# Softmax attention of a long fused kernel: the products for the maxima of a head run two heads ahead of its scores, and its row of maxima is made in the middle of the head before

## The reference, cut to what matters

```python
def block_attention(q, k, v):
    ...
    scale = dh ** -0.5

    def one_block(qi):
        sc = jnp.einsum("bqgrd,bkgd->bgrqk", qi, k).astype(jnp.float32) * scale
        p = jax.nn.softmax(sc, axis=-1).astype(v.dtype)
        return jnp.einsum("bgrqk,bkgd->bqgrd", p, v)
```

## Time and profile before

| | |
|---|---|
| median of 3 runs | 1560.02 us (1559.63 to 1560.45) |
| the profiled execution | 1560.5 us |
| its span, first to last instruction | 1558.7 us |
| TensorE busy | 98% of the span |
| VectorE, ScalarE, GpSimd busy | 73%, 54%, 58% |
| granted TensorE clock, mean | 0.998 of full |

### The profile page before, as it was taken

One profiled execution on the slowest core, in us unless ns is written; L12 is line 12 of the kernel. 1 busy time (PEld: TensorE's weight loads), 2 busy tenths in 40 slices (PEclk: granted clock), 3 DMA queues, 4 the chain that ended last, 5 costly groups with the idle time before them and its releaser, 6 DMA issues.

```text
span 1558.7 us, 23051 instructions
## 1 busy us (share of the span) xinstructions
PE 1528.3 (98%) x7975; PEld 1235.0 (79%) x7975; DVE 1139.1 (73%) x1590; ACT 834.7 (54%) x1552; POOL 907.3 (58%) x644
## 2 busy tenths in 40 slices
PE   7999999999999999999999999999999999999998
PEld 4778888888878766687777888888888888888887
DVE  4799888888739888488459878877768895567542
ACT  4775765766633587423344444444458665454442
POOL 0556765766655876556846767776753467532314
PEclk9999999999999999999999999999999999999999
DMA  8434434434332300276622333333422334322212
GB/s 328 133 122 129 128 108 130 131 107 129 115 94 70 81 28 1 83 239 249 214 67 83 96 92 103 108 109 109 113 83 81 95 102 122 94 62 69 68 41 82
DMA packets 77485, 171.34 MB, mean 110 GB/s; under 512 B 8321, under 2 KB 10753, under 8 KB 73921
## 3 DMA queue, kind: packets, MB, share of 16 engines
q1 hardware_dynamic: 70064, 133.09, 28.7%
q10 hardware_dynamic: 7312, 36.83, 6.7%
HBM read 167.67 MB, written 2.23 MB: 109 GB/s over the span
## 4 chain that ended last, share of the span: by engine, by line
PE 64%; DVE 13%; issue 8%; POOL 6%; DMA 2%; ACT 2%; ACTq 0%; DVEq 0%; POOLq 0%; SPq 0%
PE bank L1401 8%; PE bank L1403 7%; PE bank L1402 7%; PE bank L1419 7%; PE bank L1422 7%; PE bank L1420 7%; POOL w_lo L716 6%; PE bank L1864 4%; DMA w_raw<-ws 2%; PE bank L1866 2%; DVE ada_acc L2155 2%; PE bank L1757 2%; DVE rstd L2454 2%; PE bank L2021 1%; PE bank L1695 1%
## 5 line engine op out<-in xcount | busy, mean ns | idle before, releaser
L716 POOL TENSOR_TENSOR w_lo<-w_raw,w_hi 128x512 fp32r<-128x512 f32 x440 | 644.8, 1489 | 403.2 <-ACT w_hi L775 402.8
L775 ACT ACTIVATE w_hi<-w_raw 128x512 fp32r<-128x512 f32 x444 | 260.4, 624 | 124.0 <-DMA w_raw<-ws 104.2
L1401 PE MATMUL bank<-a_hi_and_lo,w_hi 128*128 128x512 f32 (+1 forms) x800 | 315.8, 395 | 2.4 <-ACT gates_early L840 1.2
L1403 PE MATMUL bank<-a_hi_and_lo,w_lo 128*128 128x512 f32 (+1 forms) x800 | 308.7, 386 | 0.0
L1402 PE MATMUL bank<-a_hi_and_lo,w_hi 128*128 128x512 f32 (+1 forms) x800 | 308.3, 385 | 0.0
L1419 PE MATMUL bank<-b_hi,w_hi 128*128 128x512 f32 x536 | 210.2, 392 | 2.6 <-ACT tmp L1119 1.4
L1422 PE MATMUL bank<-b_lo,w_hi 128*128 128x512 f32 x536 | 209.2, 390 | 0.0
L1420 PE MATMUL bank<-b_hi,w_lo 128*128 128x512 f32 x536 | 209.0, 390 | 0.0
L1401 PEld LDWEIGHTS bank<-a_hi_and_lo,w_hi 128*128 128x128 f32 x800 | 150.4, 188 | 36.6 <-issue 4.4
L1402 PEld LDWEIGHTS bank<-a_hi_and_lo,w_hi 128*128 128x128 f32 x800 | 150.5, 188 | 30.8 <-issue 1.9
L1403 PEld LDWEIGHTS bank<-a_hi_and_lo,w_lo 128*128 128x128 f32 x800 | 150.3, 188 | 30.8
(11 more groups left out here) (447 smaller groups left out, 3183.2 us busy)
## 6 DMA issues: line engine op xcount, KB each, us to landing
w_raw<-ws SPq DMA_DIRECT2D x457, 256.0 KB, 2.7
cs_rows<-cs_scratch ACTq DMA_DIRECT2D x16, 1024.0 KB, 5.2
ada_piece<-ada ACTq DMA_DIRECT2D x16, 1024.0 KB, 5.3
ada_piece<-ada SPq DMA_DIRECT2D x8, 1024.0 KB, 17.6
x_stream<-x SPq DMA_DIRECT2D x2, 1024.0 KB, 8.5
x_stream<-x ACTq DMA_DIRECT2D x1, 2048.0 KB, 7.8
out<-x_stream SPq DMA_DIRECT2D x4, 256.0 KB, 3.3
out<-x_stream SPq DMA_DIRECT2D x8, 128.0 KB, 1.8
```

Source lines behind the costliest of these rows:

```text
L716: nc.gpsimd.tensor_tensor(wlo[b][:, :], full[:, :], r32(whi[b][:, :]), ALU.subtract)\
L775: A(whi[n % RING][:, :], full[:, :], ACT.Copy).then_inc(hi_done, 1)
L1401: mm(out, lh, rh, start=first, stop=False)
L1403: return mm(out, ll, rh, start=False, stop=last)
```

## The change

Three edits, on four engines' lists:

- scores_for_max and max_of run for head h + 2 in head h (AHEAD_OF), except in heads 0 and 1, where it is h + 1 as before. The four M of head 3, which no head's chunks would hold, are put between the value products of heads 0 and 1. So heads 14 and 15 hold no M.
- row_of_max(h + 1) stands in the middle of head h, between its second and third chunk, for heads 2 to 14, and max_row(h + 1) on ScalarE between the third and the fourth exponential.
- query_high(3) moves into head 0 on ScalarE, and query_low(3) into head 0 on VectorE.

```diff
+AHEAD_OF = [1, 1] + [2] * (N_Q - 2)
...
                     A(probs_of(h)[:, c, :], S[n % 2][:, :], ACT.Exp, scale=HD ** -0.5).then_inc(exp_done, 1)
+                    if c == 2 and 1 < h < N_Q - 1:
+                        max_row(h + 1)
+                    if (h, c) == (0, 1):
+                        query_high(3)
                 if h % 2 == 0:
...
-                    max_row(h + 1)
                     if h == 0:
+                        max_row(1)
...
                 else:
-                    query_high(3)
+                    max_row(2)
                 if h + 3 < N_Q:
                     query_high(h + 3)
-                if h + 1 < N_Q:
-                    max_row(h + 1)
...
                     scores(h, c)
-                    if h + 1 < N_Q:
-                        scores_for_max(h + 1, c)
+                    if h + AHEAD_OF[h] < N_Q:
+                        scores_for_max(h + AHEAD_OF[h], c)
...
-                chunks_of(h, 0, NCH)
+                chunks_of(h, 0, NCH // 2)
+                if 1 < h < N_Q - 1:
+                    row_of_max(h + 1)
+                chunks_of(h, NCH // 2, NCH)
                 if h % 2 == 0:
                     take_sums(u - 1, 0)
-                    row_of_max(h + 1)
                     take_sums(u - 1, 1)
                     continue
...
                     values(u, c)
-                    if c == 1:
-                        if h + 1 < N_Q:
-                            row_of_max(h + 1)
-                        if u:
-                            turn_inverse(u - 1)
+                    if u == 0:
+                        scores_for_max(3, c)
+                        if c == 1:
+                            row_of_max(2)
+                    elif c == 1:
+                        turn_inverse(u - 1)
...
             for h in range(N_Q):
-                if h + 1 < N_Q:
+                if h + AHEAD_OF[h] < N_Q:
                     for i in range(NCH):
-                        max_of(h + 1, i)
+                        max_of(h + AHEAD_OF[h], i)
+                if h == 1:
+                    for i in range(NCH):
+                        max_of(3, i)
...
-                if h == 1:
+                if h == 0:
                     query_low(3)
```

## The result

The changed kernel takes **1566.2 us** (median of 8 runs, 1563.2 to 1570.2), the kernel before beside it 1560.5 us (8 runs, 1559.6 to 1564.5). The ratio is 1.0034, 95% interval 1.0024 to 1.0043: slower by 5.3 us by the ratio, by 5.8 between the two medians. The sum had +4.3 and the time 1564.3, the range 1561.3 to 1566.4. The profiled execution took 1566.2 us, span 1564.4, 5.7 more than before.

A forecast was written before the change was run, and what follows sets the result against it. TensorE, almost never waiting in the attention, was taken to bound the kernel. Terms 0.3 + 1.4 + 2.9 + 0.5 - 0.8 = +4.3 us moved the median from 1560.02 to 1564.3, range 1561.3 to 1566.4.

The forecast's parts named there:

- Head 4's query is wanted in head 2: Head 2's first M of head 4 waits 2.8 us for query_low(4), and the next matmul is 0.1 longer: +2.9 us.
- The M of head 3 between values: Four M among pair 0's values cost two at 0.47 and two at 0.24, for distances and changes of kind: +1.4 us.
- The row moved: Row among scores: -0.05 us in each of six even heads (2 to 12), +0.10 in six odd (3 to 13): +0.3.
- Heads 6 and 10: Query behind turn_q: head 6's new 0.9 us wait replaces an old 0.5, +0.4; head 10 +0.1; together +0.5.
- Head 14: Head 14 loses its four M, is paced by exponentials and hides the row: 4.99 to 4.15 us, -0.8.
- the chance for the clock: Rival: the clock falls to 1.2 GHz after head 2's pause, costing 1.8 us more: +6.1, 1566.1 us; chance 0.07.
- the delay would be absorbed behind the attention: Rival: waits of 1.2 and 1.5 us after the attention take up delay, leaving +1.6, 1561.6 us; chance 0.10.

The follow-up runs named there:

- the run with the clock kept: Changed kernel plus 15 bf16 matmuls of 384 columns between head 2's first scores and head 4's first M: 1565.4 us, ratio 1.0026 to the kernel before.
- the run with the row at the end: Changed kernel, head 1's reciprocal in head 0, query_low(4) before head 3's last reduction, row_of_max and max_row back in old places from head 2: 1561.8 us, ratio 1.0009.
- the version with VectorE moved: Kernel before, TensorE's order untouched, VectorE's reciprocals of the last two query tiles in heads 0, 5, 7 and turn_q in heads 3, 8: 1564.9 us, ratio 1.0023.

## Why the prediction came out as it did

The direction and the place were right, and the time was 1.9 us too low. The range held it by 0.2 us, and that is luck: its upper end was made for a fall of the clock of 1.8 us, and two more executions of the changed kernel took 1569.0 and 1570.0. By its own steps, in the attention:

- *Head 4's query is wanted in head 2*, +2.9: measured 2.8 and 0.1 (head 2 as a whole, in the run with the clock kept, 7.71 against 4.98). Its chain was right as well: reduction, 1.75 for the reciprocal, q_lo in 0.62 and not 1.27, with GpSimd idle from 554.81 on. One reading was too kind: the q_lo of 0.69 runs from 556.85 to 557.54, so GpSimd, at work from 557.08 on, worked for two thirds of it, and it was hardly slower than the 0.62. The rule on the shared SBUF interfaces (the Trainium skill, GPSIMD Engine Reference, Specifications) agrees in direction: 0.62 with GpSimd idle, 1.27 with GpSimd at work for nine tenths of it; but the 0.69 shows that work beside it need not cost much.
- *The M of head 3 between values*, +1.4: **measured +1.8** (head 2's first scores 19.59 behind the attention's start, before 17.77). I had priced a lone M at 0.47; the rows of the changed kernel have the last value products ahead of one at 549.75, the M at 550.28 and the next values at 550.71: 0.43 for the M, and 0.53 ahead of it where the next values come after 0.42, so 0.54 together:

```profile
549.75 0.59 PE L1760 MATMUL bank<-probs,v_by_token 128*64 128x512 f32 x1
...
550.28 0.50 PE L1732 MATMUL bank<-k_hi_over_lo,q_hi_twice 128*128 128x512 f32 x1
550.71 0.64 PE L1760 MATMUL bank<-probs,v_by_token 128*64 128x512 f32 x1
```

  Two shared their changes with the row and the scores, as forecast, and cost more than the 0.24 as well: 1.8 less 2 x 0.54 leaves 0.7 for both. This is the mis-sized term.
- *The row moved*, +0.3: measured 0.07 in each of the six odd heads, where 0.10 had been forecast. Heads 4, 8 and 12 came out 0.08 shorter, forecast -0.05, but by the run with the row at the end that is not the row's doing. Together +0.2.
- *Heads 6 and 10*, +0.5: +0.44 and -0.03, with the wait at the first M 0.85 where 0.9 was forecast.
- *Head 14*, -0.8: -0.78.

The whole attention of the run with the clock kept is +4.39 (110.08 against 105.69): 2.7 for head 2, 1.8 for the M, 0.2 for the row, 0.4 and -0.8. The forecast was +4.3. So the sum was right for a pause that leaves the clock alone; that it is right to 0.1 is in part luck, since the M were 0.4 too cheap and the other terms together 0.3 too dear.

**The step that failed is the chance for the clock**, and its price. The prediction weighed 2.8 us of pause against one pause of 2.43 at the program's start behind which nothing slow was seen, and gave 0.07. All four profiles of the changed order with a pause of 2.6 or more had the fall, and even 1.82 us in the kernel before had it, both times. One case without it was no ground for 0.07, nor is a second that the trace of before held (below). Nor is the place itself safe: in the profile of the version with VectorE moved its pause was 3.12 instead of 2.43, and the clock fell there for 10.2 us. The price, 1.8, was near that of the shortest fall (1.55); it was 4.6 in the second profile.

That the delay would be absorbed behind the attention was rightly given little. From the attention's end to the span's end it takes 917.8 us before and 917.2 after, and 916.5 to 918.6 in all 14 profiles, whose attentions differ by up to 12.7 us. That the spans differ by 5.7, close to the attention's 5.94, is in part chance: ahead of the attention the profile after lost 1.55 to another fall of the clock (below), and it was 1.2 sooner past the program's start, where TensorE waits for DMA.

## What to carry to other kernels

When products are asked for earlier, look first at who makes their operands: here the row that was moved was never late, and the query that came to be wanted a head sooner was. Price a new wait of TensorE twice, its own length and then 0.45 us for each us at the lower clock behind it, which differed from one execution to the next; if the wait can't be removed, a few matmuls into a free bank can bridge it, as 15 did here. And fit long pieces of VectorE to idle stretches by length: in head 0 6.4 us of them cost nothing, in heads 3 and 8 they made waits of 1.3 and 2.3.

## What the runs showed of the hardware

- A pause of TensorE in head 2 was followed by a stretch at the lower clock in six profiles of six: 10.2 and 10.2 us for a pause of 1.82, 3.4 and 10.2 for one of 2.63, 13.7 and 3.4 for one of 4.25 (in the first of these the fall came 0.3 before the pause was over). Behind 1.02 idle there, and behind 2.27 in head 9 of another version, it did not fall, nor in any of the 14 profiles behind the wait at the mixer's products, at 102 to 107 us, which is nearly as long as the shortest above (of before):

```profile
102.93 0.44 PE L1695 MATMUL bank<-M,X_tok 128*64 128x128 f32 x4 [1.78 <-DVE M L2412]
```

  At the program's start a pause of 0.8 to 2.5 us left the clock at 1.00 in 13 profiles; in the other, of the version with VectorE moved, it was 3.12, and the clock fell about 1 us before it was over (0.88 in the window from 12 to 14, 0.50 in the next):

```profile
14.53 1.94 PE L1540 MATMUL bank<-ada_piece,small 128*32 128x256 f32 x16 [3.12 <-DMA ada_piece<-ada]
```

```profile
14.00:16.00 2.00, 1.47 (x16) 0.69 (x16) 1.76 (x3) 1.65 (x4) 0.00 (x0) 0.50 1.03 434
```

  So the length of the idle time alone does not decide; what else does, these runs don't show.

- Nor does it need a pause of that kind. Around 430 us, where in all kernels TensorE does two groups of 8 one-column matmuls with 0.47 idle between, 9 of the 14 profiles show a fall of 3.4 us, both of the changed kernel's among them, the kernel before's not:

```profile
428.00:430.00 2.00, 1.53 (x14) 1.44 (x14) 0.75 (x1) 1.96 (x4) 0.49 (x1) 1.00 0.00 0
430.00:432.00 2.00, 2.00 (x6) 1.56 (x6) 0.00 (x0) 0.00 (x0) 2.00 (x2) 0.51 0.03 9
432.00:434.00 2.00, 2.00 (x7) 1.59 (x6) 0.69 (x1) 0.63 (x1) 1.77 (x5) 0.64 0.76 196
```

From the products near 103 us to the attention it takes 433.8 to 433.9 us in the nine profiles with that fall and 432.3 in the five without, 1.55 us. That is one source of the spread of the times of each kernel, and a reason to compare a stretch inside the profiles where a difference of 1 us matters.
